# Half-groups of small matmuls at steps of their own, and one ScalarE copy at another place, in the DeltaNet part of a hybrid decoder layer

## The reference

```
kk  = k k^T ;  a = strict_lower(beta * kk * decay)
sol = solve(I + a, [beta*v , beta*exp(gc)*k])      # unit lower triangular
u_bar, w = sol
qk  = (q k^T) * decay
# scan over chunks
u     = u_bar - w state
o     = q_dec state + qk u
state = g_last*state + k_dec^T u
```

## Time and profile before

| quantity | value |
|---|---|
| median of 3 runs | 2428.38 us (2424.05 to 2431.61) |
| the profiled execution's own time | 2424.05 us |
| its span | 2422.2 us |
| PE busy | 2328.8 us (96%), 11568 instructions |
| DVE busy | 916.5 us (38%) |
| ACT busy | 697.4 us (29%) |
| POOL busy | 660.4 us (27%) |

### The profile page before, as it was taken

How to read it: one execution, slowest core, us unless ns; L and a number is a source line. 1 busy time by engine, 2 the same in 40 slices (tenths; PEclk the granted TensorE clock), 3 DMA queues, 4 the chain that set the end, 5 groups by cost and what they waited for, 6 DMA issues and landing times.

```text
span 2422.2 us, 31268 instructions
## 1 busy us (share of the span) xinstructions
PE 2328.8 (96%) x11568; PEld 1929.1 (80%) x11568; DVE 916.5 (38%) x1118; ACT 697.4 (29%) x1220; POOL 660.4 (27%) x447
## 2 busy tenths in 40 slices
PE   5999999999799999999999999998999999999998
PEld 4887878788588887888887888886888888888887
DVE  4415253444755565555543113313222112211234
ACT  4323332333454555555452210013110011100112
POOL 6352222312111111111112323332333233323231
PEclk8999999999899999999999999999999999999999
DMA  5112121202120211122023433331111111111112
GB/s 119 42 44 88 44 95 44 87 26 96 44 61 17 69 61 35 43 66 63 17 79 117 152 127 105 115 87 44 52 52 44 52 44 52 43 52 44 52 39 83
DMA packets 219107, 157.28 MB, mean 65 GB/s; under 512 B 22744, under 2 KB 205208, under 8 KB 217520
## 3 DMA queue, kind: packets, MB, share of 16 engines
q1 hardware_dynamic: 206528, 106.05, 15.7%
q10 hardware_dynamic: 12528, 50.53, 5.9%
HBM read 137.49 MB, written 19.07 MB: 65 GB/s over the span
## 4 chain that ended last, share of the span: by engine, by line
PE 87%; DVE 5%; DVEq 2%; DMA 2%; issue 2%; POOL 1%; ACT 1%; SPq 0%; ACTq 0%; POOLq 0%
PE bank L198 65%; PE bank L988 5%; PE bank L1221 2%; PE bank L1204 2%; DMA stat_b<-scr_stat 1%; DVEq L765 1%; PE bank L1159 1%; PE bank L1211 1%; PE bank L1258 1%; PE bank L602 1%; DVE joint L769 1%; PE bank L1178 1%; PE bank L1240 1%; PE bank L1184 1%; PE bank L1234 1%
## 5 line engine op out<-in xcount | busy, mean ns | idle before, releaser
L198 PE MATMUL bank<-u_hi,w_hi 128*128 128x512 f32 x2176 | 903.1, 415 | 14.3 <-DVE u_lo L1677 7.2
L198 PE MATMUL bank<-u_hi,w_lo 128*128 128x512 f32 x2176 | 852.1, 392 | 0.0
L198 PE MATMUL bank<-u_lo,w_hi 128*128 128x512 f32 x2176 | 849.3, 390 | 0.0
L184 POOL CAST w_hi<-raw 128x1024 fp32r<-128x1024 f32 (+1 forms) x176 | 184.7, 1049 | 1680.5 <-PE bank L198 1431.7
L198 PEld LDWEIGHTS bank<-u_hi,w_hi 128*128 128x128 f32 x2176 | 411.0, 189 | 89.5 <-DVE u_lo L1677 8.1
L198 PEld LDWEIGHTS bank<-u_hi,w_lo 128*128 128x128 f32 x2176 | 409.1, 188 | 88.7
L198 PEld LDWEIGHTS bank<-u_lo,w_hi 128*128 128x128 f32 x2176 | 411.3, 189 | 71.2 <-issue 3.8
L186 POOL TENSOR_TENSOR w_lo<-raw,w_hi 128x1024 fp32r<-128x1024 f32 (+1 forms) x176 | 430.1, 2444 | 25.7 <-issue 0.7
L1791 DVE TENSOR_TENSOR tmp<-tmp,bank 128x512 f32<-128x512 f32 x44 | 30.2, 687 | 367.4 <-PE bank L198 367.4
L198 PE MATMUL bank<-v_hi,w_hi 128*128 128x512 f32 x352 | 137.2, 390 | 2.6 <-DVE tmp L1791 2.6
L198 PE MATMUL bank<-v_lo,w_hi 128*128 128x512 f32 x352 | 137.0, 389 | 0.0
(11 more groups left out here) (247 smaller groups left out, 2715.8 us busy)
## 6 DMA issues: line engine op xcount, KB each, us to landing
raw<-in_w_in SPq DMA_DIRECT2D x84, 512.0 KB, 3.9
stat_b<-scr_stat ACTq DMA_DIRECT2D x12, 1024.0 KB, 7.0
row<-scr_rows ACTq DMA_DIRECT2D x24, 512.0 KB, 4.9
raw<-in_w_gate SPq DMA_DIRECT2D x22, 512.0 KB, 3.8
raw<-in_w_up SPq DMA_DIRECT2D x22, 512.0 KB, 3.9
scr_gate<-tmp ACTq DMA_DIRECT2D x16, 512.0 KB, 2.9
tmp<-scr_gate ACTq DMA_DIRECT2D x16, 512.0 KB, 4.4
raw<-in_w_down SPq DMA_DIRECT2D x16, 512.0 KB, 3.9
```

What stands on the lines that cost most here:

```text
L184: nc.gpsimd.tensor_copy(hi[:, 0:kt, :], raw[slot][:, 0:kt, :])
L198: last = nc.tensor.matmul(bank[dst][:, :], wpart[slot][wp][:, k, :], rhs[ap][:, k, half * HALF:(half + 1) * HALF], start=k == 0 and (wp, a ...
```

## The change

Two things are changed. The table `STEPS_AT` gives `vt1`, `kt1`, `kk0`, `kk1`, `qk0`, `qk1`, `t00` and `t01` steps of their own or other steps. And the copy of `a_right` on ACT moves: for level 1 from step `qk1` to the end of step `t01`; for levels 2 to 6 from the end of step `p` of the level before to the end of step `y` of the level before.

```diff
-        STEPS_AT = {4: ["ss"], 8: ["vt0", "vt1"], 15: ["kt0", "kt1", "kk0", "kk1"],
-                    17: ["qk0", "qk1"], 19: ["t00", "t01"], 41: ["tt0", "tt1"], 43: ["ub0", "ub1", "wt0", "wt1"],
+        STEPS_AT = {4: ["ss"], 8: ["vt0"], 9: ["vt1"], 15: ["kt0"], 16: ["kt1", "kk0"], 17: ["kk1"], 18: ["qk0"],
+                    19: ["qk1"], 20: ["t00"], 21: ["t01"], 41: ["tt0", "tt1"], 43: ["ub0", "ub1", "wt0", "wt1"],
                     62: ["os"], 63: ["on"]}
@@ delta_act, step "qk1"
                 f(z_now[:, :], z_next[:, :], ACT.Copy).then_inc(dl["z"], 1)
-                act.wait_ge(dl["a"], two + 2)
-                f(by_block(a_right[:, :], 1), side_columns(neg_a[:, :], 1, 1), ACT.Copy).then_inc(dl["ar"], 1)
@@ steps "t00", "t01"
                 f(c4(inv, half), bank[X0 + half][:, :].rearrange("p (c t) -> p c t", t=P), ACT.Copy).then_inc(dl["t0c"], 1)
+                if half == 1:
+                    act.wait_ge(dl["a"], two + 2)
+                    f(by_block(a_right[:, :], 1), side_columns(neg_a[:, :], 1, 1), ACT.Copy).then_inc(dl["ar"], 1)
@@ steps "y1" to "y6", then "p1" to "p6"
                 f(half_pair[64:P, :, 64:P], y_now[64:P, :, 64:P], ACT.Copy).then_inc(dl["yc"], 1)
-            elif step[0] == "p":
-                level = int(step[1])
-                act.wait_ge(dl["pr"], h * 6 + level)
-                f(inv_t[:, 0:HALF], bank[X0][:, :], ACT.Copy).then_inc(dl["prc"], 1)
                 if level < 6:
                     f(by_block(a_right[:, :], level + 1), side_columns(neg_a[:, :], level + 1, 1), ACT.Copy).then_inc(dl["ar"], 1)
+            elif step[0] == "p":
+                act.wait_ge(dl["pr"], h * 6 + int(step[1]))
+                f(inv_t[:, 0:HALF], bank[X0][:, :], ACT.Copy).then_inc(dl["prc"], 1)
```

## The result

| | before | after |
|---|---|---|
| median | 2429.99 us (4 runs, 2424.05 to 2431.93) | 2451.77 us (4 runs, 2450.89 to 2454.68) |
| ratio, 95% interval | | 1.0098, 1.0085 to 1.0110 |
| profiled execution, its span | 2424.05, 2422.2 us | 2451.97, 2450.2 us |

The change makes the kernel slower by some 24 us (by the interval 21 to 27 us). The forecast was slower by 15.4 us, 2444 us in a range of 2434 to 2451. The direction and the place were right, and the size was too small by a third. The time lies 0.8 us outside the range. The kernel before measured 2429.99 us this time, 1.6 us above the 2428.4 from which the range was laid, so the last step over its edge owes something to chance; that the size is wrong does not.

The account below looks back on a forecast made before the run. PE was taken to bound the kernel, so only its waits count: 0.81 + 0.51 + 4 x 0.15 = 1.92 us per head, times 8 = 15.4 us, on 2428.4 gives 2444 us, range 2434 to 2451.

Parts of the forecast that it names:

- What bounds the kernel: In the DeltaNet head loop PE is busy 82.53 of 84 us; time on DVE, ACT, POOL counts only if PE waits.
- The half-groups cost nothing in themselves: Spreading eight side steps over more steps costs PE 0.01 us per group cut in two, taken as zero; gain zero.
- The entry to `y1`: At level 1, y1 newly waits for ACT's a_right copy behind t01: 0.81 us per head, bounds 0.70 to 0.92.
- The wait of `d`: a_right now stands between half_pair and inv_t on ACT, so d starts 0.15 us later at levels 2 to 5 each.
- At level 1: ACT has no gap before inv_t here, so the whole 0.51 us goes onto d1, bounds 0.38 and 0.63.
- The upper bound: y1 and d waits at their largest: 0.92 + 0.63 + 4 x 0.26 = 2.59 us per head, 20.7 us in all.
- A: Rival: a_right fits the 0.36 us gap before inv_t at levels 2 to 5; 10.6 us lost, 2439 us; chance 0.09.
- B: Rival at step 48: PE's lag ends the collision of L1493 with POOL, returning 6.1 us; 2438 us; chance 0.06.
- C: Rival at level 4: POOL's cast starts before DVE's inv_right copy and blocks it; 23 us added, 2467 us; chance 0.03.
- D: Rival: the reordering helps unseen, such as a shorter wait at d (11.5 us); at best 2423 us; chance 0.05.
- The signs: Profile after: y1 gap 0.8 us, L1221 waits about 33 us, L1204 about 8 x 1.0, head 86 us, L1493 2.3 us.

Follow-up runs that it names:

- e1: The kernel before with the new STEPS_AT table alone, all a_right copies left in place: 2434.5 us, ratio 1.0014.
- e5: The changed kernel with a second a_right-sized copy ahead of the first at levels 2 to 6: 2472.8 us, ratio 1.0180.
- e2: The changed kernel with the old STEPS_AT table, so the moved a_right copies alone: 2446.1 us, ratio 1.0061.
- e6: The kernel before with each level's inv_t copy cut into two of 256 columns, each with its own signal: 2421.6 us, ratio 0.9962.
- e9: The changed kernel with the a_right copy of levels 2 to 6 ahead of the two half_pair copies instead of behind: 2446.6 us, ratio 1.0072.
- e7: The kernel before with halved inv_t copies as in e6 and the last eight convolution pieces two steps later, at 50 to 57: 2411.9 us, ratio 0.9924.

## Why the prediction was wrong

- **What bounds the kernel** was right: DVE and ACT have room, and every part of the loss is a wait of PE.
- **The half-groups cost nothing in themselves** was right: of e1's 0.38 us per head 0.35 are the wait of `y1` and what follows from it. The prediction had that wait inside its `y1` term; e1 shows that the table alone already uses up the cover of ACT's inv copy.
- **The entry to `y1`** was right: 0.72 us instead of 0.81, eight times, released by a_right. The copy ends 1.80 us after the four transposes start, as forecast; PE followed it sooner than by the 0.14 I had read at `d`: a_right of 1176.09 ends at 1176.76, and `y1` starts at 1176.81.
- **The wait of `d`** is the step that failed, in the sentence "a_right holds ACT for some 0.51". It took this occupancy from an overlap seen between inv_t and a_right, and used it for the pair a_right and inv_t, which the trace of before does not show. Measured: 0.65 to 0.66, and 0.40 between half_pair and a_right where I had 0.38; e5 confirms that what ACT does between half_pair and inv_t goes onto `d`, so the path was right and this term too small. Levels 2 to 5 became 0.32 each instead of 0.15, in sum 0.66 us per head.
- **At level 1** it was 0.78 instead of 0.51: 0.15 from the same error, and 0.11 because ACT's half_pair starts 1.22 after `y1` rather than 1.11. A `y1` that had to wait starts with its weight loads uncovered: before, they started 0.23 us ahead of its matmuls (1152.93 and 1153.16), now at the same time (1176.81), and L1204 takes 1.18 rather than 1.07. This was not in the forecast. It shows in e1 too, without any a_right in front of `d`.
- Together 0.66 + 0.27 - 0.09 = 0.84 us per head, 6.7 us: with 15.4 that is 22.1, against 22.5 from the heads.
- **The upper bound** failed with it. For levels 2 to 5 it took "a_right must have ended" as the worst case, 0.26. Gaps of 0.02 to 0.03 us at the two joints and 0.01 of a_right's own duration come on top, and the measured 0.32 lies above it.
- **The rivals**: A (only level 1 is hit) is refuted by e2. B's collision stayed at 2.34 us: POOL's L186 starts 0.33 us ahead of L1493 (1218.89 and 1219.22; before 0.35), which fits the argument that POOL is released by PE and moves with it. C did not come: DVE's L1390 at level 4 starts at 1192.59 and POOL's cast at 1192.79, 0.20 apart as before. D did not come, though e6 shows that the time it spoke of exists.
- **The signs**: the gap at `y1` with eight waits at L1204 (7.9 us in sum) and L1493 came as put. The waits at L1221 rose to 39.9 us instead of 33, and a head to 86.92 us instead of 86.
- The ScalarE page of the Trainium skill ("ScalarE: Activation LUTs", "What ACT_TABLE_LOAD costs") says that back-to-back ACTIVATEs overlap by about 93 ns. This case agrees for some pairs (0.09 to 0.12) and differs for a_right followed by inv_t or conv_in and for half_pair followed by anything, where the next copy starts 0 to 0.03 after the end.

## What to carry to other kernels

- An idle gap in front of a copy is cover only up to its length. Moving a copy from behind the one that a busy engine waits for to ahead of it cost what did not fit into the gap, at each place, 40 times here (five levels, eight heads), though the engine that does it is half idle.
- The distance between two instructions belongs to the pair. Where the trace does not show the new pair, take the full duration and a little more as the upper bound, since full duration alone (0.62) was below what was measured (0.65).
- Where an engine waits for the end of one copy, it can pay to cut that copy in two with a signal each: here it gave 1.26 us per head (e6), and the reordering of the copies around it that was tried gave 0.69 (e9).
- Two edits that each look cheap can use up the same cover. The level-1 copy cost nothing with the old table and 0.49 us per head with the new one.
- Read a loss on PE from the starts of matmuls. The idle time shown ahead of `y1` was 0.56 where 0.72 was lost.

## What the runs showed of the hardware

- Two neighbouring ACT copies overlap by about 0.1 us or not at all, and their order has a part in it: the same four copies take 1.31 or 1.45 us to the start of the last (e9 against the changed kernel). The cause stays open.
- A group of small matmuls on PE that had to wait for its operand is itself slower at its start: `y1` hands its result to ACT 0.11 us later when it waited (1.22 against 1.11), and L1259 follows a waiting L1258 0.11 us later (0.33 in e6 against 0.22 in e7).
- DVE's L1493 beside POOL's L186 takes 2.34 us, and 0.48 behind it. Moving it two steps was worth 1.12 us per head, more than the 0.87 of the single gap on PE that the trace of before shows: 1.01 between starts, and 0.11 for the slower start.
